# Grouping the wide and the narrow products of the projections, with the inverse roots and both ends of the program reordered

## The chip, the cores and the metric

The kernel runs on one core of one Trainium2 chip. The metric is the device time of the program in microseconds, as the median of several runs. Engines: TensorE (PE) multiplies, PEld is its weight load, VectorE (DVE), ScalarE (ACT) and GpSimd (POOL) do elementwise work, SyncE (SP) issues nearly all DMA transfers. The engines run their own instruction streams and meet at semaphores.

## The reference, cut to what matters

Two transformer-like blocks over 256 tokens of width 1024, one after the other, all in float32:

```python
# block one
xn = rmsnorm(x);  h = xn @ w_in            # 10 parts: recurrent unit, gates, q, k, v, index heads
x = x + merged @ w_out                      # recurrent branch and sparse attention, gated
up = rmsnorm(x) @ w_up                      # 2 x 3072
x = x + (gelu(conv(up[:, :3072])) * up[:, 3072:]) @ w_down
x = x + sigmoid(rmsnorm(x) @ w_ple_gate) * (p @ w_ple_proj)
# block two
x = x + 0.5 * (silu(g) * u) @ ffn1_w_out    # g, u = split(rmsnorm(x) @ ffn1_w_in), 2816 each
x = x + merged @ w_o                        # two attentions
x = x + 0.5 * (silu(g) * u) @ ffn2_w_out    # the same again
return rms_norm(x, final_norm)
```

## The kernel before

**Layout and precision.** Features lie on the 128 partitions, the 256 tokens (T) on the free axis, so x is 8 tiles (K = 8) of 128 x 256. Every float32 operand is split into a high part, rounded to the fp32r type, and a low part, the rest. A product W x is three: high by high, high by low, low by high. ScalarE rounds a weight unit from `raw` into `wh` (`round_unit`), VectorE subtracts to get `wl` (`rest_unit`), and the semaphore `rest` counts finished units.

**Units.** Weights come in units of 2048 columns per partition (half that in the down projections), in a ring of three (RING). SyncE loads a unit when the `rest` of the unit three before is done. The order of the units is the table UNIT_COUNTS: the input projection of block one (KI, QI, K, V, Q, LX, LG, RI, GA, GB), YB, YA, WO, then UP1 and DN1 (24 up units, 24 down pieces), PR and PG (the gate), UP2 and DN2, the second block's input projection (20 units), its branches and WO2, UP3 and DN3. UP2 and UP3 have 22 units.

**Two ways of multiplying.** `three` and `half_pair` do the three products with 256 columns each. `split_product` does two: wh by high and low side by side, 512 columns into a whole PSUM bank, then wl by high, 256 columns into its left half. Left and right half are added afterwards. The up projections (`split_pair`, 16 pairs a unit: 8 k by 2 output tiles), the down projections except their last output tile (`one(c)` with c < 7), and most of WO and WO2 do so. For each k the 512-column product is followed at once by the 256-column one:

```python
mm(ps, w, both.rearrange("p h t -> p (h t)"), start=first, stop=False)
return mm(ps[:, 0:T], wl[:, slot, w0:w0 + P], both[:, 0, :], start=False, stop=last)
```

**The inverse root of a norm.** For the norms 1, 3 and 5 the up projection starts on the unscaled x. `up_first_two` multiplies the first unit, sums the squares on TensorE with `sum_added` before the unit's last two pairs, and then, between the first unit and the second, `spread_inv` waits for `diag_done` and multiplies ones by a diagonal. In between ScalarE takes the root (`rms_root`), VectorE the reciprocal and the diagonal (`norm_diag`). ScalarE's `copy_inv` then copies the result, and VectorE scales with it.

**Key norm.** In the first block `key_spread` does the like for the keys; it stands behind `pair(5)` and ahead of `dots(4)` and `pair(6)`.

**Gate.** After DN1, ScalarE's order is: evacuate PR 0 and 1, `norm_high(2)`, evacuate PR 2 and 3, round the second gate unit (U["PR"] + 2).

**Start.** TensorE waits for all four constants of GpSimd, does two warming products (`keep_clock(2)`), transposes the gain and x (four groups e of 4 transposes), with `keep_clock(e)` behind groups 1 and 3, and then the 72 columns of KI and unit 1. ScalarE squares tokens, makes all 8 high tiles (`gained_high(0, 8)`) and then rounds KI. SyncE loads x, units 0 to 2, many small parameters one by one, with the K unit between them (it waits for `rest` of KI), and then V.

**End.** After DN3, VectorE makes the 8 gained tiles, TensorE transposes them (groups f of 4, the last sum of squares between f = 1 and f = 2), ScalarE copies the four results with the inverse root as a scale, and SyncE stores each.

Of the kernel before, what the change touches and what calls it, by code (L numbers as in the profile page):

```python
# [25 lines left out]
ALU = mybir.AluOpType  # L26
# [166 lines left out]
def build(nc, A, onehots, out):  # L193
    with ExitStack() as ctx:
# [55 lines left out]
        fin_banks = [banks[1], banks[3], banks[5], banks[0]]  # L250
# [83 lines left out]
        fin_turned, fin_copied, stored = sem("fin_turned"), sem("fin_copied"), sem("stored")  # L334
# [43 lines left out]
        def _(sp):  # L378
# [139 lines left out]
            for h in range(2):  # L518
                for i in range(2):
                    sp.wait_ge(fin_copied, 2 * h + i + 1)  # L520
                    sp.dma_start(o[:, i, h * 512:(h + 1) * 512], xtok[:, i, h * 512:(h + 1) * 512]).then_inc(stored, 16)
# [39 lines left out]
        def _(act):  # L561
# [69 lines left out]
            gained_high(0, 8)  # L631
            round_unit(0)
            round_half(1, 0, early_round)
# [363 lines left out]
            norm_high(2)  # L997
            for m in range(2, 4):
                evac(group(U["PR"]) + m, page_g[:, 2 * m:2 * m + 2, :])
            round_unit(U["PR"] + 2)  # L1000
# [197 lines left out]
        def _(dve):  # L1198
# [469 lines left out]

            def ffn_down(name, scale, n=None):
# [103 lines left out]
            for k in range(K):  # L1773
                dve.wait_ge(read_d, READ_BY["D"][group(U["DN3"])] + k + 1)
                dve.tensor_scalar(page_g[:, k, :], x[:, k, :], param("final_norm_2", k), None, ALU.mult).then_inc(xn_done, 1)
# [629 lines left out]
```

## Time and profile before

| | |
|---|---|
| median of 3 runs | 1060.05 us (1059.98 to 1060.81) |
| profiled execution, its own time | 1064.18 us |
| profiled execution, span of the instructions | 1062.4 us |
| TensorE busy | 1050.5 us, 7128 products |
| VectorE busy | 769.4 us |
| ScalarE busy | 580.5 us |
| GpSimd busy | 184.0 us |
| DMA | 186.97 MB, 176 GB/s |
| mean granted TensorE clock | 0.999 |

The span runs from the first instruction to the last; the rest of the own time lies outside it. Products overlap in the pipeline, so their printed durations add up to more than the time that they take; the distance between starts is their pace.

### The profile page before, as it was taken

The page shows a single profiled execution, that of the slowest core. Times are in us where ns is not written, and L with a number is a line of the kernel's source. Part 1 is how long each engine was busy: PE and PEld are TensorE (multiplying, and loading weights), DVE is VectorE, ACT ScalarE, POOL GpSimd, SP SyncE. Part 2 cuts the span into 40 slices and gives each one's busy share as a digit, 9 for nine tenths or more (in the row PEclk, how much of TensorE's full clock was granted, in tenths as well). Part 3 has the DMA queues.
Part 4 walks back from the last instruction along what each step waited for, and adds up shares of the span by engine and source line. Part 5 has one row for each costly group of instructions (what it writes and reads, how often), then busy time and mean ns, then how long its engine had stood idle before and what let it go on. Part 6 is the DMA issues. An engine that isn't in the chain of part 4 may idle for free.

```text
span 1062.4 us, 18504 instructions
## 1 busy us (share of the span) xinstructions
PE 1050.5 (99%) x7128; PEld 960.9 (90%) x7128; DVE 769.4 (72%) x945; ACT 580.5 (55%) x810; POOL 184.0 (17%) x209
## 2 busy tenths in 40 slices
PE   9999999999999999999999999999999999999997
PEld 8899999998888888899888888999999988888887
DVE  5799875648999996468777765666665687787552
ACT  5745799346656554367544454546566365444442
POOL 0300000222321220022322220010000223222200
PEclk9999999999999999999999999999999999999999
DMA  8744366645766757466766575654444466664751
GB/s 258 217 141 157 120 206 200 229 159 160 197 183 174 196 158 222 137 193 190 195 179 192 148 204 164 221 181 154 159 148 154 136 170 195 190 193 140 213 166 40
DMA packets 289747, 186.97 MB, mean 176 GB/s; under 512 B 6703, under 2 KB 286326, under 8 KB 289686
## 3 DMA queue, kind: packets, MB, share of 16 engines
q1 hardware_dynamic: 289566, 186.02, 59.7%
q8 instruction: 44, 0.72, 0.3%
q14 instruction: 17, 0.14, 0.0%
q10 hardware_dynamic: 120, 0.09, 0.0%
HBM read 184.94 MB, written 1.08 MB: 175 GB/s over the span
## 4 chain that ended last, share of the span: by engine, by line
PE 92%; DVE 3%; ACT 2%; DMA 1%; SPq 1%; issue 0%; ACTq 0%; DVEq 0%
PE psum L1794 36%; PE psum L1831 20%; PE psum L1795 18%; PE psum L1787 4%; PE psum L1789 4%; PE psum L1788 4%; DVE wl L1213 1%; PE psum L1890 1%; PE psum L1857 1%; PE psum L1891 1%; PE psum L1892 1%; ACT wh L567 1%; PE psum L2077 1%; DMA raw<-in_w_in 1%; PE psum L2105 1%; ACT parts L601 1%
## 5 line engine op out<-in xcount | busy, mean ns | idle before, releaser
L1794 PE MATMUL psum<-parts,wh 128*128 128x512 f32 x1628 | 576.9, 399 | 0.0
L1213 DVE TENSOR_TENSOR wl<-raw,wh 128x2048 fp32r<-128x2048 f32 (+3 forms) x210 | 415.3, 1995 | 107.6 <-ACT wh L567 107.4
L1795 PE MATMUL psum<-parts,wl 128*128 128x256 f32 x1628 | 457.2, 281 | 0.0
L1794 PEld LDWEIGHTS psum<-parts,wh 128*128 128x128 f32 x1628 | 306.0, 188 | 76.3 <-DVE wl L1213 0.5
L567 ACT ACTIVATE wh<-raw 128x2048 fp32r<-128x2048 f32 (+3 forms) x211 | 330.0, 1584 | 47.2 <-PE psum L1789 36.1
L1795 PEld LDWEIGHTS psum<-parts,wl 128*128 128x128 f32 x1628 | 307.6, 189 | 0.1
L1831 PE MATMUL psum<-parts,wh 128*128 128x256 f32 x1376 | 252.3, 285 | 0.2 <-DVE wl L1213 0.2
L1831 PEld LDWEIGHTS psum<-parts,wh 128*128 128x128 f32 x1376 | 214.7, 192 | 3.1 <-issue 2.0
L1831 PE MATMUL psum<-parts,wl 128*128 128x256 f32 x688 | 194.3, 283 | 0.0
L924 ACT ACTIVATE page_q<-psum 128x512 f32<-128x512 f32 x68 | 40.6, 597 | 167.4 <-PE psum L1795 167.4
L1831 PEld LDWEIGHTS psum<-parts,wl 128*128 128x128 f32 x688 | 131.9, 192 | 0.0
L1787 PE MATMUL psum<-parts,wh 128*128 128x256 f32 x324 | 92.8, 287 | 0.1
L1789 PE MATMUL psum<-parts,wl 128*128 128x256 f32 x324 | 91.7, 283 | 0.0
L1788 PE MATMUL psum<-parts,wh 128*128 128x256 f32 x324 | 91.7, 283 | 0.0
L1151 POOL CAST parts<-page_g 128x256 f32 x68 | 39.8, 585 | 296.2 <-DVE page_g L1645 296.2
L1606 DVE TENSOR_TENSOR page_x<-psum,page_q 128x512 f32<-128x512 f32 x68 | 46.7, 687 | 41.1 <-ACT page_q L924 41.1
L1153 POOL TENSOR_TENSOR parts<-page_g,parts 128x256 f32 x68 | 62.6, 921 | 12.0 <-POOL parts L1151 11.8
L1787 PEld LDWEIGHTS psum<-parts,wh 128*128 128x128 f32 x324 | 62.1, 192 | 0.8 <-issue 0.6
L1788 PEld LDWEIGHTS psum<-parts,wh 128*128 128x128 f32 x324 | 62.1, 192 | 0.3 <-issue 0.2
L1789 PEld LDWEIGHTS psum<-parts,wl 128*128 128x128 f32 x324 | 62.1, 192 | 0.0
L980 ACT ACTIVATE page_y<-x 128x256 f32<-128x256 f32 x24 | 9.9, 412 | 71.1 <-DVE x L1684 62.7
L1678 DVE SCALAR_TENSOR_TENSOR x<-psum,x 128x256 f32<-128x256 f32 x24 | 10.1, 423 | 45.2 <-PE psum L1795 35.9
(244 smaller groups left out, 947.2 us busy)
## 6 DMA issues: line engine op xcount, KB each, us to landing
raw<-in_ffn_w_in SPq DMA_DIRECT2D x88, 512.0 KB
raw<-in_w_in SPq DMA_DIRECT2D x24, 1024.0 KB
raw<-in_w_up SPq DMA_DIRECT2D x48, 512.0 KB
raw<-in_w_mix_in SPq DMA_DIRECT2D x20, 1024.0 KB
raw<-in_ffn_w_out SPq DMA_DIRECT2D x32, 448.0 KB
raw<-in_w_down SPq DMA_DIRECT2D x24, 512.0 KB
raw<-in_ffn_w_out SPq DMA_DIRECT2D x16, 512.0 KB
raw<-in_w_attn_br SPq DMA_DIRECT2D x4, 1024.0 KB
```

The lines of the kernel that those rows point to most:

```text
L567: act.activation(place(wh, u), place(raw, u), ACT.Copy).then_inc(rounded, 1)
L924: act.activation(page_q[:, 2 * j:2 * j + 2, :], low_part(RING_BASE[j]), ACT.Copy).then_inc(low_copied, 1)
L1151: pool.tensor_copy(high, src).then_inc(hi_done, 1)
L1153: pool.tensor_tensor(low, src, high.bitcast(F32), ALU.subtract).then_inc(lo_done, 1)
L1213: dve.tensor_tensor(place(wl, u), place(raw, u), place(wh, u).bitcast(F32), ALU.subtract).then_inc(rest, 1)
L1606: dve.tensor_tensor(page_x[:, 2 * j:2 * j + 2, :], main_part(RING_BASE[j]), page_q[:, 2 * j:2 * j + 2, :], ALU.add).then_inc(read_d, 1)
L1787: mm(ps, w, high, start=first, stop=False)
L1788: mm(ps, w, low, start=False, stop=False)
L1789: return mm(ps, wl[:, slot, w0:w0 + P], high, start=False, stop=last)
L1794: mm(ps, w, both.rearrange("p h t -> p (h t)"), start=first, stop=False)
L1795: return mm(ps[:, 0:T], wl[:, slot, w0:w0 + P], both[:, 0, :], start=False, stop=last)
L1831: ins = mm(bank(group(u))[:, s * T:(s + 1) * T], w, (low if j == 1 else high)[:, t0 + k, :], start=(k == 0 and j == 0), stop=(k == K - 1 a ...
```

## The change

It touches four places.

1. `both_halves` replaces the alternation: all 512-column products of a unit (the two output tiles in turn for each k), then all 256-column ones. The down projection does the same within each piece of 7 or 8 tiles for c < 7.
2. `spread_inv` moves from between the first and second up unit to behind k = 0 and 1 of the second. In the first unit only k = 7 of the second output tile is left behind the sum.
3. `key_spread` moves behind `dots(4)` and half of `pair(6)`; the second gate unit is rounded ahead of the evacuation of PR 2 and 3.
4. Start: the constants come in another order and TensorE waits for the first alone, then warms with 4 products, then 1 behind group 1; KI is rounded behind 4 of the 8 high tiles; unit 1 starts with the products that need only wh. VectorE makes the diagonal before a half of unit 1's wl. End: each gained tile is made when its x is done, and VectorE does two of the four copies, with a semaphore of its own.

```diff
-            gained_high(0, 8)
+            gained_high(0, 4)
             round_unit(0)
+            gained_high(4, 4)
...
             norm_high(2)
+            round_unit(U["PR"] + 2)
             for m in range(2, 4):
                 evac(group(U["PR"]) + m, page_g[:, 2 * m:2 * m + 2, :])
-            round_unit(U["PR"] + 2)
...
-            for f in range(4):
-                act.wait_ge(fin_turned, f + 1)
-                h, i = f // 2, f % 2
-                act.activation(xtok[:, i, h * 512:(h + 1) * 512], fin_banks[f][:, :], ACT.Copy, scale=rms[:, i:i + 1]).then_inc(fin_copied, 1)
+            for h in range(2):
+                act.wait_ge(fin_turned, 2 * h + 1)
+                act.activation(xtok[:, 0, h * 512:(h + 1) * 512], fin_banks[2 * h][:, :], ACT.Copy, scale=rms[:, 0:1]).then_inc(fin_copied, 1)
...
+            pool.memset(ones[:, :], 1.0).then_inc(consts, 1)
             pool.memset(ident[:, :], 0.0).then_inc(pool_seq, 1)
-            pool.memset(ones[:, :], 1.0).then_inc(consts, 1)
...
+            norm_diag(0)
             rest_half(1, 1, rest, rounded, 2)
-            norm_diag(0)
...
                     add(c)
+                    if name == "DN3":
+                        final_tile(c)
...
+            dve.wait_ge(inv_done, 7)
+            for h in range(2):
+                dve.wait_ge(fin_turned, 2 * h + 2)
+                dve.tensor_scalar(xtok[:, 1, h * 512:(h + 1) * 512], fin_banks[2 * h + 1][:, :], rms[:, 1:2], None,
+                                  ALU.mult).then_inc(fin_copied_d, 1)
...
+            def both_halves(u, base, both, t0=0, ks=range(K), before=None):
+                for k in ks:
+                    if before:
+                        before(k)
+                    for s in range(2):
+                        w = k * 256 + s * P
+                        mm(banks[base + s], wh[:, u % RING, w:w + P], both[:, t0 + k, :, :].rearrange("p h t -> p (h t)"),
+                           start=(k == 0), stop=False)
+                for k in ks:
+                    for s in range(2):
+                        w = k * 256 + s * P
+                        ins = mm(banks[base + s][:, 0:T], wl[:, u % RING, w:w + P], both[:, t0 + k, 0, :],
+                                 start=False, stop=(k == K - 1))
+                return ins
...
-                split_half(u, 0, base, both, t0)
-                split_half(u, 1, base, both, t0).then_inc(mm_done, 1)
+                both_halves(u, base, both, t0).then_inc(mm_done, 1)
...
+                both_halves(u, RING_BASE[0], both, t0, range(6), input_ready)
+                both_halves(u, RING_BASE[0], both, t0, (6,), input_ready)
+                split_half(u, 0, RING_BASE[0], both, t0, input_ready, (7,))
                 sum_added(n)
-                split_half(u, 1, RING_BASE[0], both, t0, ks=(6, 7)).then_inc(mm_done, 1)
+                split_half(u, 1, RING_BASE[0], both, t0, ks=(7,)).then_inc(mm_done, 1)
+                unit_ready(u + 1)
+                pe.wait_ge(signal, readers[before + (4 if n == 3 else 3)])
+                both_halves(u + 1, RING_BASE[1], both, t0, range(2))
                 spread_inv(n)
-                pe.wait_ge(signal, readers[before + (4 if n == 3 else 3)])
-                split_pair(u + 1, RING_BASE[1], 0, both, t0)
+                both_halves(u + 1, RING_BASE[1], both, t0, range(2, K)).then_inc(mm_done, 1)
...
-            pe.wait_ge(consts, CONSTS)
-            keep_clock(2)
+            pe.wait_ge(consts, 1)
+            keep_clock(4)
+            pe.wait_ge(consts, CONSTS)
...
-                if e % 2:
-                    keep_clock(e)
+                if e == 1:
+                    keep_clock(1)
...
             pair(5)
-            key_spread()
             dots(4)
-            pair(6)
+            pair(6, between=key_spread)
...
+                        for ks in (range(nk),) if c < 7 else ():
+                            for k in ks:
+                                if c == 0 and r == 2:
+                                    pe.wait_ge(lo_done, lows + k0 + k + 1)
+                                mm(ps, wh[:, u % RING, w0 + k * P:w0 + k * P + P],
+                                   hidden[:, k0 + k, :, :].rearrange("p h t -> p (h t)"), start=(k0 + k == 0), stop=False)
+                            for k in ks:
+                                ins = mm(ps[:, 0:T], wl[:, u % RING, w0 + k * P:w0 + k * P + P], hidden[:, k0 + k, 0, :],
+                                         start=False, stop=(k0 + k == sum(pieces) - 1))
```

## Rows read from the trace of the kernel before

**Rows 1.** Head of the page: engine, busy us, share of the span, instructions.

```profile
PE 1050.5 (99%) x7128; PEld 960.9 (90%) x7128; DVE 769.4 (72%) x945; ACT 580.5 (55%) x810; POOL 184.0 (17%) x209
```

**Rows 2.** The chain that ended last, share of the span by engine.

```profile
PE 92%; DVE 3%; ACT 2%; DMA 1%; SPq 1%; issue 0%; ACTq 0%; DVEq 0%
```

**Rows 3.** Timeline, TensorE, in UP1: start, duration, instruction [idle before].

```profile
359.74 0.40 PE L1794 MATMUL psum<-parts,wh 128*128 128x512 f32 x1
359.98 0.28 PE L1795 MATMUL psum<-parts,wl 128*128 128x256 f32 x1
360.09 0.40 PE L1794 MATMUL psum<-parts,wh 128*128 128x512 f32 x1
...
365.39 0.40 PE L1794 MATMUL psum<-parts,wh 128*128 128x512 f32 x1
```

**Rows 4.** The page's groups: count, busy us, mean ns.

```profile
L1794 PE MATMUL psum<-parts,wh 128*128 128x512 f32 x1628 | 576.9, 399 | 0.0
```

**Rows 5.** The chain in order of time: start, us. 256 columns fp32r; 512 columns fp32.

```profile
162.19 23.04 PE psum L1831 x192
...
825.11 1.72 PE psum L2362 x4
```

**Rows 6.** Timeline, TensorE: products with weights of 72 columns.

```profile
11.69 1.10 PE L2019 MATMUL psum<-parts,wh 128*72 128x256 f32 x8
...
12.62 1.10 PE L2022 MATMUL psum<-parts,wl 128*72 128x256 f32 x8
```

**Rows 7.** TensorE's timeline at the key spread, and the chain before it.

```profile
45.76 2.20 DVE wl L1213
...
50.77 0.70 PE L1978 MATMUL psum<-root,ones 128*128 128x512 f32 x1 [1.59 <-DVE root L1347]
```

**Rows 8.** Timeline, TensorE: the spreads of the three up stages.

```profile
261.69 0.70 PE L1964 MATMUL psum<-root,ones 128*128 128x256 f32 x2 [0.36 <-DVE root L1227]
...
498.65 0.70 PE L1964 MATMUL psum<-root,ones 128*128 128x256 f32 x2 [0.64 <-DVE root L1227]
...
871.75 0.70 PE L1964 MATMUL psum<-root,ones 128*128 128x256 f32 x2 [0.36 <-DVE root L1227]
```

**Rows 9.** Timelines around the second gate unit, ScalarE and TensorE.

```profile
468.25 1.06 ACT L575 ACTIVATE page_g<-psum 128x512 f32<-128x512 f32 x2
...
473.49 0.39 PE L1831 MATMUL psum<-parts,wh 128*128 128x256 f32 x1 [0.24 <-DVE wl L1213]
```

**Rows 10.** Timeline, GpSimd: the last low part of UP1.

```profile
398.71 0.73 POOL L1153 TENSOR_TENSOR parts<-page_g,parts 128x256 f32 x1 [0.18 <-POOL parts L1151]
```

**Rows 11.** Windows, UP1: busy us of PE, PEld, DVE, ACT, POOL; clock; DMA.

```profile
265.00:392.00 127.00, 127.00 (x721) 110.13 (x720) 117.53 (x160) 73.05 (x90) 29.90 (x44) 1.00 0.66 182
```

**Rows 12.** The chain in order of time, from the start.

```profile
4.64 1.97 PE psum L2006 x8
6.61 0.85 PE psum L1995 x2
...
11.64 0.41 SPq L393
...
19.13 6.80 DMA raw<-in_w_in
```

**Rows 13.** Timelines of ScalarE and TensorE near 41 us.

```profile
40.37 0.62 ACT L746 ACTIVATE logit<-kt 128x512 f32<-128x512 f32 x1
...
41.03 1.05 PE L1972 MATMUL psum<-ones,logit 128*128 128x1 f32 x8
```

**Rows 14.** The chain in order of time, at the end.

```profile
1053.54 0.42 DVE x L1678
...
1055.07 1.09 PE psum L2377 x8
...
1057.18 0.69 ACT page_x L1087
...
1058.45 1.16 ACT page_x L1087 x2
```

More of the change, by code:

```diff
@@ L249, in build @@
         turned_x = (banks[3], banks[4], banks[5], banks[6])
-        fin_banks = [banks[1], banks[3], banks[5], banks[0]]
+        fin_banks = [banks[1], banks[3], banks[5], banks[4]]
         table1 = nc.dram_tensor("table1", (8, REL), F32).ap()
@@ L1667, in ffn_up, with final_tile @@
                 product(n_hidden - 1)
+            def final_tile(k):
+                dve.wait_ge(read_d, READ_BY["D"][group(U["DN3"])] + k + 1)
+                dve.tensor_scalar(page_g[:, k, :], x[:, k, :], param("final_norm_2", k), None, ALU.mult).then_inc(xn_done, 1)
             def ffn_down(name, scale, n=None):
@@ L1822, in unit_ready, with half_pair @@
                 pe.wait_ge(rest, u + 1 + 3 * i3)
-            def half_pair(u, s, passes=(0, 1, 2), before=None, high=xh, low=xl, t0=0):
+            def half_pair(u, s, passes=(0, 1, 2), before=None, high=xh, low=xl, t0=0, final=2):
                 for k in range(K):
@@ L1831, in half_pair @@
                         ins = mm(bank(group(u))[:, s * T:(s + 1) * T], w, (low if j == 1 else high)[:, t0 + k, :],
-                                 start=(k == 0 and j == 0), stop=(k == K - 1 and j == passes[-1] and 1 in passes))
+                                 start=(k == 0 and j == 0), stop=(k == K - 1 and j == final))
                 return ins
@@ L1866, in first_pairs, with pair @@
                     split_half(v, 1, OUT_BASE[m], both, t0).then_inc(mm_done, 1)
-            def pair(u, i3=0, free=True, parts=(xh, xl, 0)):
+            def pair(u, i3=0, free=True, parts=(xh, xl, 0), between=None):
                 unit_ready(u, i3)
@@ L1875, in pair @@
                 half_pair(u, 0, **x_parts)
+                if between:
+                    between()
                 half_pair(u, 1, **x_parts).then_inc(mm_done, 1)
@@ L2019, in _ @@
                 mm(bank(0)[0:72, 0:T], wh[:, 0, w[k]], hl[:, 16 + k, :], start=False, stop=False)
+            raw_parts = dict(zip(("high", "low", "t0"), unscaled(0)))
+            pe.wait_ge(early_round, 1)
+            half_pair(1, 0, (0, 1), **raw_parts)
             unit_ready(0)
@@ L2023, in _ @@
             ins.then_inc(mm_done, 1)
-            raw_parts = dict(zip(("high", "low", "t0"), unscaled(0)))
             pe.wait_ge(early_half, 1)
-            half_pair(1, 0, **raw_parts)
+            half_pair(1, 0, (2,), **raw_parts)
+            pe.wait_ge(rounded, 2)
+            spread_inv(0)
+            half_pair(1, 1, (0, 1), **raw_parts)
             unit_ready(1)
-            spread_inv(0)
-            half_pair(1, 1, **raw_parts).then_inc(mm_done, 1)
+            half_pair(1, 1, (2,), **raw_parts).then_inc(mm_done, 1)
             pair(2, parts=unscaled(0))
@@ L2268, in one @@
                             pe.wait_ge(lo_done, lows + k0 + nk)
-                        for k in range(nk):
-                            if c == 0 and r == 2:
-                                pe.wait_ge(lo_done, lows + k0 + k + 1)
+                        for k in range(nk) if c == 7 else ():
                             first, last = k0 + k == 0, k0 + k == sum(pieces) - 1
-                            if c == 7:
-                                ins = three(ps[:, 0:T], u % RING, w0 + k * P, hidden[:, k0 + k, 0, :], hidden[:, k0 + k, 1, :], first, last)
-                            else:
-                                ins = split_product(ps, u % RING, w0 + k * P, hidden[:, k0 + k, :, :], first, last)
+                            ins = three(ps[:, 0:T], u % RING, w0 + k * P, hidden[:, k0 + k, 0, :], hidden[:, k0 + k, 1, :], first, last)
+                        for ks in (range(nk),) if c < 7 else ():
[7 more added lines that the diff above has]
+                                         start=False, stop=(k0 + k == sum(pieces) - 1))
                         ins.then_inc(mm_done, 1)
```

16 lines of the change are left out of this document (6 added, 10 removed).

## The prediction

> **What bounds the kernel.** I read the head of the page first: TensorE is busy 1050.5 us, 99% of the span [rows 1], and the chain that ended last runs through it for 92% [rows 2]. So only two things can move the time: the pace of the product stream, and the few places where TensorE stands still. The pace comes from the timeline. In the up and down projections a product of 512 columns (wh, both halves of the input) alternates with one of 256 (wl); sixteen such pairs start between 359.74 and 365.39, so a pair takes 0.353 us [rows 3], and there are 1628 of them [rows 4], 575 us of the span. The reader should not take the printed durations (0.40 and 0.28) for the pace: products overlap, and where only 256-column products run, 192 of them take 23.04 us, 0.120 each [rows 5].
>
> The stops come from the timeline's "idle before" column. A 256-column row is printed 0.28 long, though the next could start after 0.12, so a true stop is the printed idle plus 0.16. That gives five stops that the change addresses: 1.59 + 0.16 = 1.75 us before the key spread [rows 7], 0.52, 0.80 and 0.52 before the three spreads of the inverse roots in the up stages [rows 8], and 0.40 ahead of the second gate unit [rows 9]. The head and the tail of the program are read from the chain.
>
> **The grouping of products.** Up units but the first of a stage, all but the last output tile of each down projection, and the third unit of the two output products now run all 512-column products, then all 256-column ones. Of 1628 pairs, 32 stay alternating in the first two output units and 6 (k = 7 of three first units): 1590 are regrouped. No instruction is added or removed, so all depends on the slot of each kind among its own. For 256 it is known: 0.120 [rows 5]. For 512 columns among themselves the trace has no row. Between two readings I take this one: the pair is 0.353, less 0.120 leaves 0.233 for the 512. A check: 256-column products with weights of only 72 columns run at (12.62 - 11.69) / 8 = 0.116 [rows 6], and twice that is 0.233 again. So the stream seems to cost in proportion to its columns, the extra 3 to 4 ns of the 0.120 being the full-width weight load, and the order changes nothing: 0.233 + 0.120 = 0.353, cost 0.
>
> Bounds. Below: a column of the two-pass fp32 products runs at 1.72 us / 4 / 2 = 0.215 per 512 [rows 5]; with 0.120 that is 0.335, a gain of 18 ns a pair, 29 us in all. Above: if a 512 among its own needed two of the 0.120 slots, 0.240 + 0.120 = 0.360, a loss of 7 ns a pair, 11 us. I take zero, since the nearest rows are products of the same type (rows 6) and not fp32.
>
> The regrouping also moves when inputs are needed. In the first output tile of a down projection the last hidden tile's product now starts 7 x 0.233 into its piece instead of 7 x 0.353. UP1's last low part is ready at 398.71 + 0.73 = 399.44 [rows 10]; the down projection starts near 392.2 (23 units of 16 x 0.353 behind the first spread of rows 8, which ends about 262.2), so it is needed at 392.2 + 16 x 0.353 + 1.63 = 399.5 instead of 400.3. It just fits; I charge 0.1. VectorE in UP1 is busy 117.5 of 127.0 us [rows 11], 5.2 of each 5.65 us unit, so it follows a TensorE that is unchanged or up to 7% faster. ScalarE and GpSimd are further from full there.
>
> **Inverse roots spread later.** The spread is issued after four 512 and four 256 products of the next unit: 4 x 0.353 = 1.41 us, and the sum of squares itself comes one pair later. TensorE would reach it 1.41 us later than now, while the diagonal it waits for is late by 0.35 at most. Stops of 0.52 and 0.80 are both covered, so 0.52 + 0.80 + 0.52 = 1.84 goes. Behind it ScalarE's copy of the inverse comes 0.6 to 0.9 us later; it delays the first scaling by VectorE, whose idle 8% absorbs it, and with a ring of three banks TensorE asks for the result two units (11 us) later. If that cover failed, the cost would be those 0.9 us once a stage.
>
> **Key spread inside a unit.** The same dots and half of the next Q unit run first. TensorE ends its unit at 49.0; VectorE has that next unit's wl since 45.76 + 2.20 = 47.96 [rows 7], so nothing else holds it, and the diagonal of 50.7 comes while it multiplies. The 1.75 us goes. VectorE is the busiest behind it up to 115 us, but its own work starts no later than before, and its attention work waited for TensorE.
>
> **Gate unit.** ScalarE rounds the second gate unit before two evacuations that take 1.06 us [rows 9]; its wl is ready 1.06 earlier, the stop of 0.40 goes. The evacuations end at about 471.2, before their bank is wanted at 473.
>
> **The start.** Sum of squares and KI's rounding are reordered, the warming products go from 2 + 1 + 3 to 4 + 1, and 16 products of unit 1 run ahead of the wl of unit 0. TensorE will look better there. But the chain of the start does not lie on it: from x's transposes it goes through ScalarE and VectorE's wl of KI to SyncE, which at 11.64 may issue the K load, then fourteen small loads, then the V load at 19.13, which lands at 25.9 [rows 12]. ScalarE then works without a pause that TensorE could shorten until the squares of the keys at 40.37 + 0.62 = 40.99, and TensorE's next product but one starts at 41.03 [rows 13]. What TensorE gains before 41 is waited away there. What counts is when KI's wl is ready: four warming products before the gain's transpose push it and x's transposes by about 0.5 us (8 passes of 0.43 against 4, two passes being 0.85 [rows 12]), and KI's rounding (0.68) now stands before half of the gained tiles; against that the transposes run at half the pace of those at the end (eight in 1.97 against 1.09 us [rows 12, 14]) and may reach the upper clock level sooner. I take 0.3 us of loss; the two ends are 0.5 gain and 0.8 loss.
>
> **The end.** After the last sum of x (done 1053.96 [rows 14]) the eight normed tiles are no longer all to be made: seven exist. The eight transposes that ran from 1055.07 start at 1053.75 and end at 1054.62; the last square (1054.4) is in, the sum, root and reciprocal follow as now, and the first copy starts at 1055.8 instead of 1057.18: 1.35. VectorE takes two of the four copies, each 0.69 [rows 14], so the last store, now issued at about 1059.6 after three copies at 0.58 spacing, is held only by the pace of issue. SyncE issued 15 loads between 11.64 and 19.13, 0.50 each [rows 12]: first issue 1056.5, last 1058.0. Together 1.6. Its bounds are 1.2 (copies and issues get in each other's way) and 1.8.
>
> **Sum.** 1.75 + 1.84 + 0.40 + 1.6 - 0.3 - 0.1 = 5.2 us. The profiled execution took 1064.18 us, 1.8 more than its span and 4.1 more than the median of the runs; the stops are the same work in any execution, so the 5.2 is taken from the median: 1060.05 - 5.2 = **1054.9 us**.
>
> **Rivals**, all in the 512-column slot, which multiplies by 1590:
> - Mild loss, chance 0.20. The two starts within a pair are 0.236 and 0.117 apart on average, printed as 0.24 and then 0.11 [rows 3]. If the 512 truly costs 0.236 and the 256 behind it profits from a weight load made early, grouping loses that profit: 0.236 + 0.120 = 0.356, 3 ns, 4.8 us: 1059.7. For it speaks that the 72-column case is also below 0.120; against it that the start times are modelled.
> - Real loss, chance 0.06, the other side. The 0.240 slot: +7 ns, +11 us, 1065.9. It decides from 4.6 ns a pair (5.2 + 2.1 over 1590). Against it: nothing in rows 3 needs a 512 above 0.236.
> - Fixed cost per product, chance 0.25. If 0.116 is 256 columns at 2.4 GHz (0.107) plus a fixed 0.010, a 512 costs 0.223, and the pair's missing 0.010 is a charge for alternating: grouped 0.343, a gain of 15.9 us, 1039.0. For it: fp32 products show a small fixed cost (rows 5); against it, that the proportional reading needs no such charge.
> - No overhead at all, chance 0.07: 0.335 a pair, 1026. The Trainium skill (TensorE: Matmul & The Clock Gate, Back-to-back issue gap) gives N / 2.4 + 2.5 ns for a stream, 216 ns for 512 columns, with which the grouped pair would be 0.336 and the time 1027; by it 256 columns would take 109 ns, and the trace disagrees, with 116 to 120.
> - Grouping neutral, chance 0.42: the forecast, with its own range 1053.3 to 1056.5.
>
> **Range and chances.** 1038.5 to 1060.5 takes in the fixed-cost case, the forecast and most of the mild loss; outside stay the no-overhead case and about 0.1 above. A measurement here tells 0.2%, 2.1 us, from no change. Faster by more than that: 0.07 + 0.25 + 0.41 + 0.07 of the mild loss = 0.80; same 0.14; slower 0.06.
>
> **What would show it.** In the timeline of an up stage: start to start of 512-column products (0.233 right; 0.236 or more, or 0.223 or less, one of the rivals) and of the 256 behind them (0.120). No idle ahead of the four spreads and the second gate unit. The squares' product still near 41 us. First copy of the end 1.9 us behind the last sum of x (1053.96) instead of 3.2. The prediction is wrong mainly if the 512 slot is not 0.233: each nanosecond is 1.6 us.

## The result, and the profile after

The changed kernel takes 1053.29 us (median of 4 runs, 1052.84 to 1054.05), the kernel before 1060.43 beside it (4 runs, 1059.98 to 1062.09): ratio 0.993, 95% interval 0.9916 to 0.9943. It is 7.1 us faster; 5.2 were forecast. The direction and the range were right; the gain was 1.9 us short, the time 1.6. That the time came so near is luck: it hides two wrong terms that go against each other, and a property of the old kernel that one profile could not show.

The head of the page of the changed kernel reads like [rows 1]; the chain that ended last does not read like [rows 2]:

```profile
PE 1041.7 (99%) x7126; PEld 961.1 (91%) x7126; DVE 771.0 (73%) x947; ACT 580.2 (55%) x808; POOL 183.4 (17%) x209
```

```profile
PE 80%; DVE 11%; issue 3%; ACT 3%; DMA 1%; SPq 1%; DVEq 0%; ACTq 0%
```

VectorE went from 3% of the chain to 11%: somewhere TensorE now waits for it, although TensorE's busy share is 99% in both. TensorE's timeline shows the pace of the grouped units, in UP2 (start, duration, instruction):

```profile
523.90 3.82 PE L1820 MATMUL psum<-parts,wh 128*128 128x512 f32 x16
527.56 2.08 PE L1825 MATMUL psum<-parts,wl 128*128 128x256 f32 x16
529.47 2.91 PE L1820 MATMUL psum<-parts,wh 128*128 128x512 f32 x12
```

A unit starts every 5.57 us, 16 pairs of 0.348; sixteen alternating pairs took 5.65 [rows 3]. Start to start, 512-column products are 0.2285 apart in the up stages (most of them 0.227) and 0.231 in the down stages, 256-column ones 0.1195 and 0.119. So the slot is neither the 0.233 of the forecast nor the 0.223 of its fixed-cost rival.

The spreads of the inverse roots have nothing in front of them any more (compare [rows 8]), and neither has the second gate unit ([rows 9]). Two new stops stand elsewhere: ahead of unit 8, and in the first output tile of DN1.

```profile
63.85 0.95 PE L2001 MATMUL psum<-ones,logit 128*128 128x1 f32 x8
65.73 0.50 PE L1854 MATMUL psum<-parts,wh 128*128 128x256 f32 x2 [0.93 <-DVE wl L1213]
...
261.44 0.64 PE L1825 MATMUL psum<-parts,wl 128*128 128x256 f32 x4
261.92 0.60 PE L1993 MATMUL psum<-root,ones 128*128 128x256 f32 x2
...
392.10 2.14 PE L2310 MATMUL psum<-parts,wh 128*128 128x512 f32 x8 [0.15 <-DVE wl L1213]
394.08 1.10 PE L2313 MATMUL psum<-parts,wl 128*128 128x256 f32 x8
396.57 1.66 PE L2310 MATMUL psum<-parts,wh 128*128 128x512 f32 x6 [1.39 <-DVE wl L1213]
```

VectorE's timeline says why. At 63.39 it turns to unit 8 directly behind the eight instructions of choose(0); in UP1 it makes one wl every 5.71 us, paced by its own work and by a wait of 0.25 for ScalarE's tap, while TensorE's grouped unit takes 5.57 (the same 5.71 stands in the trace of before, where TensorE's unit took 5.65):

```profile
63.39 2.28 DVE L1213 TENSOR_TENSOR wl<-raw,wh 128x2048 fp32r<-128x2048 f32 x1
...
300.93 2.28 DVE L1213 TENSOR_TENSOR wl<-raw,wh 128x2048 fp32r<-128x2048 f32 x1
...
305.20 1.52 DVE L1635 SCALAR_TENSOR_TENSOR logit<-page_x,prm,logit 128x255 f32<-128x255 f32 x2 [0.25 <-ACT logit L947]
306.64 2.28 DVE L1213 TENSOR_TENSOR wl<-raw,wh 128x2048 fp32r<-128x2048 f32 x1
```

Where the time went is read by lining up the same products of the two traces, counted from the last one, and noting how much earlier each starts in the changed kernel. This table is profile against profile (1064.18 against 1054.05), so its sum is 10.1 us and not 7.1; the experiments explain the difference.

| stretch | gain, us |
|---|---|
| start, to the first products behind the key squares | -0.33 |
| key spread | +1.86 |
| new stop ahead of unit 8 | -1.08 |
| rows of the first two units of UP1, UP2, UP3 (spreads, with some grouping) | +0.88, +1.14, +0.90 |
| rest of UP1, UP2, UP3 (grouping) | +1.91, +1.74, +1.73 |
| DN1, DN2, DN3 | -1.60, +0.60, +0.60 |
| gate unit | +0.41 |
| end | +1.39 |

At the end the first copies start 1.84 us behind the end of the last sum of x (1044.76 + 0.42), against 3.22 in [rows 14]:

```profile
1044.76 0.42 DVE L1682 SCALAR_TENSOR_TENSOR x<-psum,x 128x256 f32<-128x256 f32 x1 [6.65 <-PE psum L1797]
...
1046.82 0.17 DVE L1780 RECIPROCAL rms<-rms 128x2 f32<-128x2 f32 x1 [1.25 <-ACT rms L590]
1047.02 1.26 ACT L1087 ACTIVATE page_x<-psum,rms 128x512 f32<-128x512 f32 x2 [0.23 <-DVE rms L1780]
1047.02 1.41 DVE L1784 TENSOR_SCALAR page_x<-psum,rms 128x512 f32<-128x512 f32 x2
```

That is 1.38 us gained, the 1.35 of the forecast. The four stores behind them are issued in 1.82 us instead of 2.06; SyncE's timeline, before and after, and then the issues of each with their size and median us to landing:

```profile
1057.90 2.06 SPq L521 DMA_DIRECT2D out<-page_x  x4
...
1047.73 1.82 SPq L521 DMA_DIRECT2D out<-page_x  x4
```

```profile
out<-page_x SPq DMA_DIRECT2D x4, 256.0 KB, 2.2
...
out<-page_x SPq DMA_DIRECT2D x4, 256.0 KB, 2.5
```

The last issue ends 1.6 us earlier behind the sum of x, but the stores take 0.3 us longer to land, so 1.4 of the 1.6 is left.

### The profile page after: what moved, and what is told of

The parts are those of the page before. It is cut to its first block, busy times and chain, and to the rows that moved or that the text cites. A ratio compares the mean times of both kernels' runs of the same rounds, so it can differ in the third digit from the quotient of the medians.

```text
span 1052.2 us, 18502 instructions
## 1 busy us (share of the span) xinstructions
PE 1041.7 (99%) x7126; PEld 961.1 (91%) x7126; DVE 771.0 (73%) x947; ACT 580.2 (55%) x808; POOL 183.4 (17%) x209
## 3 DMA queue, kind: packets, MB, share of 16 engines
HBM read 184.94 MB, written 1.08 MB: 177 GB/s over the span
## 4 chain that ended last, share of the span: by engine, by line
PE 80%; DVE 11%; issue 3%; ACT 3%; DMA 1%; SPq 1%; DVEq 0%; ACTq 0%
PE psum L1854 20%; PE psum L1820 16%; PE psum L2310 10%; PE psum L1825 9%; DVE wl L1213 5%; PE psum L2313 5%; PE psum L1795 4%; PE psum L1796 4%; PE psum L1797 4%; DVE logit L1635 1%; DVE page_x L1606 1%; DMA raw<-in_w_in 1%; ACT logit L947 1%; DVE page_x L1618 1%; PE psum L1802 1%
## 5 line engine op out<-in xcount | busy, mean ns | idle before, releaser
L1820 PE MATMUL psum<-parts,wh 128*128 128x512 f32 x1114 | 267.6, 391 | 0.0
L1820 PEld LDWEIGHTS psum<-parts,wh 128*128 128x128 f32 x1114 | 204.5, 188 | 39.9 <-DVE wl L1213 0.5
L1854 PEld LDWEIGHTS psum<-parts,wh 128*128 128x128 f32 x1376 | 213.8, 192 | 5.0 <-issue 2.5
L1854 PE MATMUL psum<-parts,wl 128*128 128x256 f32 x688 | 192.0, 283 | 0.0
L1825 PEld LDWEIGHTS psum<-parts,wl 128*128 128x128 f32 x1114 | 143.7, 191 | 6.0
L1825 PE MATMUL psum<-parts,wl 128*128 128x256 f32 x1114 | 145.5, 283 | 0.0
L1854 PEld LDWEIGHTS psum<-parts,wl 128*128 128x128 f32 x688 | 130.9, 192 | 0.0
L2310 PE MATMUL psum<-parts,wh 128*128 128x512 f32 x476 | 120.3, 393 | 1.5 <-DVE wl L1213 1.5
L2310 PEld LDWEIGHTS psum<-parts,wh 128*128 128x128 f32 x476 | 85.4, 189 | 17.4 <-DVE wl L1213 1.9
L1797 PE MATMUL psum<-parts,wl 128*128 128x256 f32 x324 | 91.7, 283 | 0.0
L2313 PEld LDWEIGHTS psum<-parts,wl 128*128 128x128 f32 x476 | 65.4, 190 | 4.9
L2313 PE MATMUL psum<-parts,wl 128*128 128x256 f32 x476 | 66.9, 282 | 0.0
L1795 PEld LDWEIGHTS psum<-parts,wh 128*128 128x128 f32 x324 | 62.1, 192 | 0.6 <-issue 0.5
```

Of the source, the lines that this page charges most:

```text
L1795: mm(ps, w, high, start=first, stop=False)
L1797: return mm(ps, wl[:, slot, w0:w0 + P], high, start=False, stop=last)
L1820: mm(banks[base + s], wh[:, u % RING, w:w + P], both[:, t0 + k, :, :].rearrange("p h t -> p (h t)"), start=(k == 0), stop=False)
L1825: ins = mm(banks[base + s][:, 0:T], wl[:, u % RING, w:w + P], both[:, t0 + k, 0, :], start=False, stop=(k == K - 1))
L1854: ins = mm(bank(group(u))[:, s * T:(s + 1) * T], w, (low if j == 1 else high)[:, t0 + k, :], start=(k == 0 and j == 0), stop=(k == K - 1 a ...
L2310: mm(ps, wh[:, u % RING, w0 + k * P:w0 + k * P + P], hidden[:, k0 + k, :, :].rearrange("p h t -> p (h t)"), start=(k0 + k == 0), stop=False)
```

## The experiments

The twelve kernels were run in three sets of four; a set ran on one chip and shares its runs of the kernel before. Times are medians with their lowest and highest.

### The kernel before once more

> The kernel before, unchanged, once more with a profile. The profiled execution of before took 1064.18 us, 3.8 above the median of its runs, while that of the changed kernel took 1054.05 against 1053.29. Theory A (chance of one execution): the times agree with before (ratio 1.000), the new profiled execution lies within 1 us of the median, and its product slots are not longer than 0.353 us a pair. Theory B (the profile costs this kernel some 4 us): the profiled execution is near 1064 again. Under A, part of the 10.2 us between the two profiles is no gain of the change, and I have to find where those 3 us lie.

1063.97 us (1059.27 to 1065.60, 11 runs), before beside it 1064.38 (1061.79 to 1065.80, 17 runs), ratio 0.9996 (0.9987 to 1.0005). Theory B falls: the profiled execution took 1059.27 this time. Theory A holds in the ratio, but that execution lies 4.7 us from the median and not within 1; the spread of 6 us is the find. In the new profile the alternating stream of UP2 has another pace than in [rows 3]; TensorE's timeline:

```profile
519.70 0.39 PE L1794 MATMUL psum<-parts,wh 128*128 128x512 f32 x1
519.93 0.27 PE L1795 MATMUL psum<-parts,wl 128*128 128x256 f32 x1
520.05 0.40 PE L1794 MATMUL psum<-parts,wh 128*128 128x512 f32 x1
...
525.25 0.39 PE L1794 MATMUL psum<-parts,wh 128*128 128x512 f32 x1
```

Sixteen pairs in 5.55 us, 0.347 each. Grouped by stretches of 25 us, all pairs lie at one of two paces and at nothing between, but for the stretch in which the pace changes: 353.3 ns (starts 241, 120, 236, 113, 233, 117 ns apart, and again) or 346.7 ns (for instance 232, 118, 231, 112). In this execution DN1 (behind its first output tile), UP2 and DN2 ran at 346.7, UP1, UP3 and DN3 at 353.3. The pace is kept until a start comes late or other products stand between, and a small delay can be enough: in DN1 it changed at 400.00 us, where one start came 0.05 us late. A delay of 0.03 us at 400.72 in the first profile changed nothing. The profile that I predicted from had 353.3 everywhere. Lined up with it, the new one gains 4.2 us over the three stages at 346.7 and 0.7 at the start, together the 4.9 between 1064.18 and 1059.27. Of the runs at 1060 there is no trace; a share of pairs at 346.7 would explain them. All of them would be worth 1628 x 6.6 ns = 10.7 us.

### The grouping taken away, and the grouping alone

```diff
-                        for ks in (range(nk),) if c < 7 else ():
+                        for ks in [(k,) for k in range(nk)] if c < 7 else ():
...
+                for s in range(2):
+                    for k in ks:
+                        if before and s == 0:
+                            before(k)
+                        ins = split_product(banks[base + s], u % RING, k * 256 + s * P, both[:, t0 + k, :, :], k == 0, k == K - 1)
```

> The changed kernel with its products in the old alternating order (512, 256, 512, ...) in all three up and down projections; every other edit stays. Theory A (milestones of the two traces): grouping saves 5.0 ns on each of 1088 pairs of the up stages and 3.7 on each of some 470 of the down stages, 7.2 us, of which 2.2 are lost in the first tile of DN1; so this kernel takes about 5.0 us more than the changed one, 1058.3, and the stop of 1.39 us at the first tile of DN1 is gone. Rival (the blind forecast: grouping is worth 0): 1053.3. Second rival (the other edits bring 1.84 + 0.40 + 1.4 + 0.45 - 0.33 = 3.8 us of the 7.1): 1057.0.

1059.58 us (1056.70 to 1060.33, 6 runs), ratio to before 0.9951 (0.9937 to 0.9965). 5.4 more than the changed kernel in the next set (1054.16), 6.3 more than on record: theory A (5.0) fits, the blind forecast of 0 falls. Both stops in DN1 are gone. Its profile has DN1 at 346.7 and the rest at 353.3, and its runs spread over 3.6 us, so the two paces come with the order, though 1.5 us of the spread is clock, as the kernels below show. Between its trace and that of before, the three spreads give 0.65, 0.93 and 0.65, together 2.23, the gate 0.40, the end 1.38.

> The kernel before with the grouping alone (up units behind the first of a stage, all down tiles but the last). Theory A: 5.0 us less than before, 1055.4; the first tile of DN1 waits for VectorE as in the changed kernel. Rival (grouping worth 0): 1060.4. Second rival (3.3 us, what the other edits leave of 7.1): 1057.1. If k2 and this one give the same size, the edits add up.

1057.18 us (1056.73 to 1057.77, 5 runs), ratio 0.9934 (0.9922 to 0.9947): 7.2 less than before in this set, 2.2 more than the 5.0 of theory A. That fits a kernel before that ran mostly at 353.3 here (its median is 1064.38), which is argued from its times. The spread is 1.0 us. The changed kernel is 3.0 below it: the other edits bring 4.5 in the table, and 1.3 of that goes in DN1, where this kernel loses 0.28 and the changed one 1.60. The edit is the one that the change makes in the up and down stages, without the new place of the spreads.

### Which bank, and how long a run

```diff
-                for k in ks:
-                    for s in range(2):
+                for s in range(2):
+                    for k in ks:
```

> The changed kernel, but the 512-column products of an up unit run eight into one bank, then eight into the other, instead of changing bank at each product; the 256-column ones too. Theory A (the bank is what makes the slot 0.228 us in the up stages and 0.231 in the down stages): the slot here is 0.231, +2.5 ns x 1088 = +2.7 us, 1056.0. Rival (the bank does not matter, the down stages differ by their weights' tile, 128x1024 halves): slot 0.228, 1053.3.

1054.97 us (1054.09 to 1055.67, 5 runs), ratio 0.991 (0.9897 to 0.9922). The slot is 0.2285 as in the changed kernel: the bank does not matter, theory A fell, and the rival stands. Its profiled execution is 1.6 us longer than that of the changed kernel for another reason, seen in the windows of TensorE (busy, granted clock, DMA share, GB/s) around the stop ahead of unit 8, here and in the changed kernel:

```profile
65.00:69.50 4.50, 3.65 (x18) 0.63 0.56 170
```

```profile
65.00:69.00 4.00, 3.27 (x27) 1.00 0.54 158
```

Behind the stop, 16 products start 0.213 us apart instead of 0.120: they run at the lower of the two clock levels (1.2 instead of 2.4 GHz), 16 x 0.094 = 1.5 us. The alternating kernel shows the same at the same place.

```diff
                     for s in range(2):
                         mm(banks[base + s], wh[...], ..., start=(k == 0), stop=False)
-                for k in ks:
                     for s in range(2):
                         ins = mm(banks[base + s][:, 0:T], wl[...], ..., start=False, stop=(k == K - 1))
```

> The changed kernel with its up stages in twos: 512, 512, 256, 256 and again, where the changed kernel has sixteen and sixteen; the down stages stay grouped. Products that alternate one by one were seen at two steady paces, 353.3 ns and 346.7 ns a pair, each kept from one stop to the next, while the grouped units take 348. Theory A (each change of kind costs the same, whatever the length of a run): half of the loss of the slow pace, 350.6 ns, so 1088 x 2.6 = 2.8 us more than the changed kernel. Theory B (the pace is a lock of starts to one another, and each order has locks of its own): one steady pace per stage again, somewhere between 346.7 and 353.3, and possibly another one in another execution; then -1.4 to +5.7 us against the changed kernel.

1054.93 us (1054.24 to 1055.47, 6 runs), ratio 0.992 (0.9901 to 0.994). Its four starts (512, 512, 256, 256) are 232.9, 233.3, 114.6 and 115.9 ns apart in the mean, 348.4 a pair, the same in all stages. Theory A (350.6) fell. Theory B fits, one steady pace between 346.7 and 353.3, and no second one was seen. Runs of two are already as good as runs of sixteen; its profile, like that of the kernel just above, has the half-clock products at 65 us, and its time is the same.

### The changed kernel once more

> The changed kernel, unchanged, with a second profile, on the same chip as the others of this call. Theory A (the two paces belong to the alternating order alone): its times spread over 1.5 us or less, 1053 to 1054.5, while those of the kernel before spread over some 5 us; every up stage again has 512-column slots of 0.228 us. Theory B (the chip of the last call was slower for every kernel): this one is 4 us above 1053.3 where before is. If the stop at 65 us (1.07 us, TensorE waits for unit 8's wl) is followed by 256-column products at 0.213 us, as in two traces of the last call, 1.6 us of clock loss come with it in some executions.

1054.16 us (1053.79 to 1055.47, 6 runs), before in this set 1064.03 (1057.08 to 1066.58, 17 runs), ratio 0.9918 (0.9898 to 0.9938). Theory A: the times of the changed kernel lie within 1.7 us, those of before within 9.5. Four of the six are at 1053.8 to 1054.2 and two at 1055.4, as far apart as the half-clock products are long; the profiled one, 1054.22, has none. The two long runs have no trace, but the mean granted clock of every run is on record: 0.997 and 0.998 for these two, 0.999 or more for the other four. The kernel just above splits in the same way: 1054.24 to 1054.62 at 0.999, 1055.24 to 1055.47 at 0.997 or 0.998. So what parts the groups is time at the lower clock level; where in the run it lay is not shown.

### The stop ahead of unit 8

```diff
-            find_top(0, range(8))
-            choose(0)
-            rest_unit(8)
+            find_top(0, range(0, 4))
+            rest_unit(8)
+            find_top(0, range(4, 8))
+            choose(0)
```

> The changed kernel, but VectorE makes unit 8's wl in the middle of its first search for the top scores instead of behind choose(0), some 3 us earlier. Theory A (the gain of the key spread was eaten by this stop): the stop of 1.07 us at 65 us goes, and no product there runs at half the clock: 1.1 us less than the changed kernel, 2.7 less where that had the clock loss. Rival (VectorE is the bound of this stretch, so the wait only moves to unit 9 or 10, or to the first attention product at 91 us): 0 to 0.3 us less.

1054.81 us (1052.55 to 1055.74, 6 runs), ratio 0.992 (0.9899 to 0.9941): no gain in the median. Yet the stop is gone from its trace and nothing waits in its place up to DN1: between 60 and 73 us this trace loses 0.0 to before, the changed kernel 1.08. What it gained was lost earlier. TensorE's timeline and windows of this kernel:

```profile
41.97 1.05 PE L2002 MATMUL psum<-ones,logit 128*128 128x1 f32 x8 [0.77 <-ACT logit L747]
...
45.16 0.41 PE L1855 MATMUL psum<-parts,wl 128*128 128x256 f32 x1
45.37 0.63 PE L1855 MATMUL psum<-parts,wh 128*128 128x256 f32 x2
```

```profile
40.00:44.00 4.00, 3.23 (x26) 0.94 0.61 195
44.00:47.00 3.00, 3.00 (x15) 0.51 0.70 203
```

Before the key squares TensorE idled longer than in the changed kernel (0.77 against 0.31), then the granted clock was 0.51 for 3 us. So the 1.1 us are real in the trace, but this execution lost 2.1 us to the changed kernel's before 50 us, 0.6 by its later start and the rest with the clock. The granted clocks on record say that it was not alone: five of the six runs are at 0.997, and the one at 0.999 took 1052.55, against 1053.79 to 1054.22 for the changed kernel's runs without the loss. One run is little; the last experiment settles it.

### VectorE's round in UP1, twice

```diff
+                    if with_conv and not isinstance(i, int):
+                        rest_unit(U[name] + r + 3, i)
+                        other_taps(r, i)
+                        return
```

> The changed kernel, but in the loop of UP1 VectorE makes the wl of unit r + 3 ahead of the two taps of the convolution instead of behind them, so that ScalarE's first tap is ready without the wait of 0.25 us that it has in each unit; the last three units keep their order. Theory A (VectorE's own round of 5.70 us against TensorE's 5.565 uses up its lead over 21 units and makes the two stops, 0.31 and 1.55 us, in the first tile of DN1): the round falls to 5.45, wl is never late, 1.5 to 1.9 us less than the changed kernel. Rival (the stops come from the order of work at the end of UP1, four rounds of 4.47 us and two memsets of 0.76, whatever the lead): less than 0.4 us.

1060.70 us (1060.04 to 1062.50, 12 runs), ratio 0.9977 (0.9964 to 0.999): 6.5 more than the changed kernel, where both theories had less. It is a miss. VectorE and ScalarE now wait for each other in every unit:

```profile
294.44 2.29 DVE L1213 TENSOR_TENSOR wl<-raw,wh 128x2048 fp32r<-128x2048 f32 x1 [0.56 <-ACT wh L567]
...
300.52 2.29 DVE L1213 TENSOR_TENSOR wl<-raw,wh 128x2048 fp32r<-128x2048 f32 x1 [0.54 <-ACT wh L567]
```

```profile
292.18 0.42 ACT L940 ACTIVATE page_x<-logit 128x256 f32<-128x256 f32 x1 [2.29 <-DVE logit L1635]
292.50 1.90 ACT L567 ACTIVATE wh<-raw 128x2048 fp32r<-128x2048 f32 x1
```

ScalarE rounds the next wh behind its activation, the activation waits for the taps, and the taps now stand behind the whole wl: from the end of the taps 0.42 + 1.90 us pass on ScalarE, while VectorE has 1.86 us of other work. The round grew to 6.08 us, and TensorE stopped in each unit from 339 us on, when its lead was used up.

```diff
...
+                        dve.tensor_tensor(a[:, 0:cut], b[:, 0:cut], c[:, 0:cut], ALU.subtract)
+                        other_taps(r, i)
+                        dve.tensor_tensor(a[:, cut:], b[:, cut:], c[:, cut:], ALU.subtract).then_inc(rest, 1)
```

> The changed kernel, but in the loop of UP1 the first 512 of the 2048 columns of VectorE's wl are made ahead of the two taps (some 0.6 us) and the other 1536 behind them, so the wait of 0.25 us for ScalarE's tap is filled, while ScalarE's next rounding is delayed by no more than 0.35 us, against 1.6 us that it is ahead. Theory A (VectorE's round of 5.70 us is what makes TensorE stop in the first tile of DN1): the round falls to 5.52, under TensorE's 5.565, the stops of 0.31 and 1.55 shrink by what the lead regains, 18 x 0.13 = 2.3, so both go, but VectorE's last product of UP1 still bounds the end of the tile: 1.0 to 1.9 us less than the changed kernel. Rival (the same as with wl before the taps: the round grows through ScalarE's rounding behind the taps): the round is over 5.70 and the time rises by more than 1 us.

1051.74 us (1051.34 to 1053.54, 6 runs), ratio 0.9885 (0.9864 to 0.9905): 2.4 less than the changed kernel's 1054.16 of the other set, a little more than the 1.0 to 1.9 of theory A, which holds. The round is 5.45 us and the wait for the tap is filled (VectorE), and DN1's first tile runs through (TensorE):

```profile
298.55 0.68 DVE L1658 TENSOR_TENSOR wl<-raw,wh 128x512 fp32r<-128x512 f32 x1
...
304.00 0.69 DVE L1658 TENSOR_TENSOR wl<-raw,wh 128x512 fp32r<-128x512 f32 x1
```

```profile
391.97 2.00 PE L2318 MATMUL psum<-parts,wh 128*128 128x512 f32 x8
393.81 1.11 PE L2321 MATMUL psum<-parts,wl 128*128 128x256 f32 x8
394.76 2.19 PE L2318 MATMUL psum<-parts,wh 128*128 128x512 f32 x8
```

Over DN1 this trace gains 0.53 us on before where the changed kernel loses 1.60: 2.1 us, the whole loss. The third row is 0.19 longer than the first (2.19 against 2.00), though both are eight products: two starts come 0.07 and 0.10 us late, around 396.4, where GpSimd's last low part of UP1 is done.

### Alternating with the banks changing

```diff
+                for k in ks:
+                    for s in range(2):
+                        ins = split_product(banks[base + s], u % RING, k * 256 + s * P, both[:, t0 + k, :, :], k == 0, k == K - 1)
```

> The changed kernel with its up stages in the alternating order 512, 256, 512, 256, but with the bank changing after each pair (the kernel before stays in one bank for eight pairs). The down stages stay grouped. Theory A (the alternating order locks by chance into 346.7 or 353.3 ns a pair at each stop, whatever the banks): each up stage shows one of these two paces, and the time is -1.4 to +5.8 us against the changed kernel. Theory B (the two paces come from writing one bank all the time): a pace of its own, the same in all three stages. If it is always 346.7, this order beats grouping by 1.3 ns x 1088 = 1.4 us.

1058.00 us (1057.73 to 1058.25, 6 runs), ratio 0.9942 (0.9921 to 0.9962). All three up stages are at 353.3, and the runs spread over 0.5 us: as theory B says the pace is the same in all stages, but it is the longer of the two known ones and none of its own. TensorE does not stop in DN1 here, though the down stages are grouped: with up units of 5.65 us VectorE's 5.71 are fast enough. So the shorter pace was seen only where alternating products stay in one bank, and what chooses it there stays open.

### The start taken back

```diff
-            pe.wait_ge(consts, 1)
-            keep_clock(4)
             pe.wait_ge(consts, CONSTS)
+            keep_clock(2)
...
-            pe.wait_ge(early_round, 1)
-            half_pair(1, 0, (0, 1), **raw_parts)
             unit_ready(0)
...
```

> The changed kernel with the start of the kernel before (2, then 1 and 3 warming products; KI rounded behind all eight gained tiles; norm diagonal behind the second half of unit 1; no products of unit 1 ahead of KI's wl). Theory A (the new start costs 0.6 to 0.7 us: over seven profiles of the new start the first dots behind the key squares begin at 41.98 to 43.03, 42.47 in the mean, over three of the old one at 41.56 to 42.10, 41.8): 0.6 us less than the changed kernel. Theory B (the stop of 0.1 to 1.1 us at 41 us, which the old start has at 0.1 to 0.3, is what turns into half-clock products at 44 or 65 us in some executions): the lower of the two groups of times, 1.6 us apart, becomes the rule, so up to 1.6 us less. Rival (the start is off the path): no difference.

1053.63 us (1053.35 to 1055.49, 6 runs), ratio 0.9904 (0.9883 to 0.9925); the changed kernel had 0.9918 in another set, so the times do not tell. Over all traces, the products behind the key squares start 0.26 us later than in the first profile of before with the new start (mean of eight; k7, whose clock had fallen there, left out) and 0.05 earlier with the old one (mean of five, the last experiment's included), but single traces of either lie from 0.6 later to 0.5 earlier. A loss of 0.3 fits and is not proved. Theory B fell: one of these runs is at 1055.5 too, with a granted clock of 0.998, and the stop ahead of unit 8 is still there.

### Three edits together

> The changed kernel with three edits of these experiments together: the old start, unit 8's wl earlier, and the split wl in UP1. If they add up: 0.6 (start) + 1.1 (stop at 65 us) + 1.0 to 1.9 (first tile of DN1) = 2.7 to 3.6 us less than the changed kernel, and without the stop at 65 no half-clock products there, so 1050 to 1051 us with a spread under 1 us. Rival (VectorE between 55 and 91 us and the end of UP1 are the bounds, so that what is gained is waited away there): less than 1 us.

1050.90 us (1050.69 to 1051.15, 6 runs), ratio 0.9875 (0.9854 to 0.9895): faster than both kernels, 3.3 us less than the changed kernel (1054.16) and inside the 2.7 to 3.6 expected. Its trace is 3.2 us ahead of that of the changed kernel, 0.1 at the start, 1.1 at unit 8 and 2.1 in DN1: they add up. The chain that ended last is TensorE's again, even more than in [rows 2]:

```profile
PE 95%; ACT 2%; DMA 2%; DVE 1%; SPq 0%; issue 0%; DVEq 0%
```

Its six runs lie within 0.5 us; one or two runs of the changed kernel (second time), of the old start and of the split wl, which all have the stop ahead of unit 8, lie 1.2 to 1.4 us above the rest of theirs.

## Why the prediction was right in its direction, and where its steps failed

- **The grouping, sized 0: wrong.** The step that failed is "the order changes nothing: 0.233 + 0.120 = 0.353". The split of the pair into 0.233 and 0.120 was arithmetic, not a slot that the trace showed, and the check against the 72-column products only repeated its assumption. Measured: 0.2285 + 0.1195 = 0.348 in the up stages, 0.231 + 0.119 = 0.350 in the down stages. Against the profile of before that is 5.3 ns on 1088 pairs and, unrounded, 3.7 on 476, 7.5 us; the table has 7.3 and the 0.5 of DN1 itself. The truth fell between the neutral case, which was the forecast (0.353), and the fixed-cost rival (0.343); the measured 1053.29 lies at the lower edge of the 1053.3 to 1056.5 that the neutral case was given, but not by its mechanism. The no-overhead rival fell too. The Trainium skill (TensorE: Matmul & The Clock Gate, Back-to-back issue gap) has N / 2.4 + 2.5 ns, 216 ns for 512 columns, and calls it there the gap of an isolated product; for a stream in which each product has its weight load it has 131 ns at 512 columns. Neither agrees with this case: grouped, the products start 227 ns apart at the closest that is steady, 11 ns above the first figure.
- **The base: wrong in a way that one profile hides.** The prediction took "the same work in any execution" and moved the 5.2 us from the profile to the median of the runs. That holds for stops, not for the pace: the profile was at 353.3 ns a pair throughout, the second profile of the same kernel in part at 346.7, and the runs on record must have been so too, as far as their times tell. The grouped kernels are at 348 in every trace. So the gain is 10.1 us against the profiled execution, 7.1 against the runs on record and 9.9 against those of the second set.
- **"VectorE follows a TensorE that is up to 7% faster": wrong.** The row used, 117.5 busy of 127.0 us [rows 11], counts work and not the wait of 0.25 us in each unit, which is part of VectorE's own round: 5.71 us, slower than TensorE's unit before (5.65) and after (5.57). Each unit costs TensorE's lead 0.06 us before and 0.14 after; over 21 units the lead lasted before, and after it did not. The first tile of DN1, charged with 0.1 for the last low part, lost 2.1, and for another reason: wl. The low part was sized about right, 0.19 in the trace of the split wl. The split wl shows the cause, the alternating up units with grouped down units confirm it, and the moved wl shows how tight the ring of the two engines is.
- **Key spread, 1.75: right where it stood (1.86), then 1.08 given back.** "Its own work starts no later than before" was true and beside the point: TensorE came earlier to unit 8, whose wl stands behind choose(0). The stall was not removed but moved behind the next late thing. Moving that wl removes it, as the trace of that experiment and the time of the last one show.
- **Inverse roots, 1.84: right mechanism, 2.23 measured.** The stops were sized by printed idle plus 0.16; the second of the two spread products came 0.105 late as well each time, and 3 x 0.105 of the missing 0.39 is that.
- **Gate unit, 0.40: right (0.40, 0.41).**
- **End, 1.6: right up to the stores, 1.4 measured.** The first copies start 1.84 us behind the end of the last sum of x, just as forecast, and the last issue comes 1.6 earlier. The missing 0.2 lies behind it: the stores landed in 2.5 us (median) instead of 2.2. Why they did is not shown.
- **Start, -0.3: fits (-0.31 over all traces), inside their scatter.** TensorE's stop ahead of the key squares shows that what it gained earlier was waited away, as said.

All terms, profile against profile: the forecast's other than grouping 4.5 (1.9 - 1.1 + 2.2 + 0.4 + 1.4 - 0.3) against 5.3 forecast, and grouping 7.8 less 2.1 of its own wait, 5.7, against -0.1; together 10.2, with the rounding of the terms. The medians differ by 3.0 less: that of before lies 3.8 below its profiled execution, that of the changed kernel 0.8 below its own. Stretches at 346.7 ns in the runs of before would explain it; those runs have no trace. So profile against profile the forecast was 4.9 us short, and 3.0 of that was hidden by the base: that the time came within 1.6 us is luck.

## What to carry to other kernels

Before a stream is called neutral to its order, look at the start-to-start times over several stretches and more than one profile: a steady pair can have two paces. When TensorE gets faster, compare its new unit time with the whole round of each engine that feeds it, waits for third engines counted, and multiply the difference by the number of units; a busy share does not say it. And when a stall is removed, look up the next instruction that TensorE asks of the same engine and when that one was ready.

## What the runs showed of the hardware that was not expected

- Alternating products of 512 and 256 columns in one PSUM bank run at 353.3 or 346.7 ns a pair and stay there until a start comes late, be it by 0.05 us; with the banks changing only 353.3 was seen (one trace, six runs within 0.5 us), in runs of two 348.4, in runs of sixteen 348.0. In the twelve experiments the kernels that alternate in one bank scatter by 3.6 to 9.5 us, the others by 0.5 to 3.2 and part of either goes with the clock. What chooses the pace was not found.
- A stop of about 1 us was followed in some executions by products at half the pace (three traces with 16 at 0.213 us at 65 us, one at 44 us; granted clock 0.51 to 0.63 over windows of 3 to 4.5 us), 1.5 us on top of the stop; in others (the changed kernel, same stop, 1.00) it was not. In the second set the runs at a mean granted clock of 0.998 or less are the longer ones of each of its four kernels, by 0.9 to 2.5 us in the mean.
- One more instruction on VectorE costs little: wl in two pieces is printed 0.68 + 1.75 us against 2.28, and the round still fell by 0.26 us.
